# A mixer's elementwise work on one Trainium2 core: GpSimd's part moved to VectorE, gate units two slots after slot 2, square roots in fours

## The reference

```
p = z @ w_in_mix                       # xl | gl | u | v, 512 columns each
xc = short_conv(xl)                    # 4 taps
for direction in (forward, backward):
    r, i = sigmoid(xc @ w_r + b_r), sigmoid(xc @ w_i + b_i)   # 8 heads x 64
    log_a = -8 * r * softplus(-lam);  a = exp(log_a)
    b = sqrt(-expm1(2 * log_a)) * (i * xc)
    h = linear_scan(a, b, h0)          # h[t] = a[t] * h[t-1] + b[t]
y_lru = (h_f + h_b) * gelu(gl)
y_sgu = u * (w_s @ layernorm(v) + b_s) # chunks of 128 tokens, 4 groups
out = concat(y_lru, y_sgu) @ w_out_mix
```

## Time and profile before

| what | us |
| --- | --- |
| median of 3 runs | 1647.9 (1644.72 to 1651.6) |
| the profiled execution | 1644.98 |
| its span, first to last instruction | 1643.2 |
| TensorE busy | 1581.4 (96%) |
| VectorE busy | 975.8 (59%) |
| ScalarE busy | 630.3 (38%) |
| GpSimd busy | 176.2 (11%) |

### The profile page before, as it was taken

One profiled execution on the slowest core, in us unless ns is written; L12 is line 12 of the kernel. 1 busy time (PEld: TensorE's weight loads), 2 busy tenths in 40 slices (PEclk: granted clock), 3 DMA queues, 4 the chain that ended last, 5 costly groups with the idle time before them and its releaser, 6 DMA issues.

```text
span 1643.2 us, 24197 instructions
## 1 busy us (share of the span) xinstructions
PE 1581.4 (96%) x8838; PEld 1310.6 (80%) x8838; DVE 975.8 (59%) x1352; ACT 630.3 (38%) x838; POOL 176.2 (11%) x158
## 2 busy tenths in 40 slices
PE   5999999999999999999999999999999998799998
PEld 4788888887777787888888877888888865799997
DVE  6777777223698467773333367773333279865554
ACT  3322222222563353334322242223222247367752
POOL 0000000011343210000001010000000125320001
PEclk9999999999999999999999999999999998999999
DMA  9455556343313435552234335552334332455663
GB/s 375 145 184 186 187 180 191 127 169 114 100 61 123 154 112 173 189 192 89 100 131 153 128 97 185 182 188 89 102 129 154 128 90 90 165 208 191 191 207 114
DMA packets 84187, 249.48 MB, mean 152 GB/s; under 512 B 12704, under 2 KB 13856, under 8 KB 82976
## 3 DMA queue, kind: packets, MB, share of 16 engines
q1 hardware_dynamic: 84128, 248.71, 45.7%
HBM read 247.62 MB, written 1.05 MB: 151 GB/s over the span
## 4 chain that ended last, share of the span: by engine, by line
PE 85%; DVE 6%; issue 3%; DMA 2%; ACT 2%; POOL 2%; DVEq 0%; SPq 0%; POOLq 0%; ACTq 0%
PE bank L335 27%; PE bank L337 26%; PE bank L336 26%; DMA ada_raw<-ada_w 2%; DVE ada_acc L909 1%; PE bank L523 1%; DVE w_lo L754 1%; PE bank L355 1%; ACT z_hi L617 1%; POOL y_lo L1160 1%; DVE w_hi L983 1%; DMA res<-x_t 0%; PE bank L390 0%; DVE l_q L960 0%; DVE l_q L958 0%
## 5 line engine op out<-in xcount | busy, mean ns | idle before, releaser
L754 DVE TENSOR_TENSOR w_lo<-raw,w_hi 128x1024 fp32r<-128x1024 f32 x320 | 398.1, 1244 | 434.2 <-ACT w_hi L591 236.3
L335 PE MATMUL bank<-z_hi,w_hi 128*128 128x512 f32 (+1 forms) x1600 | 586.9, 367 | 10.5 <-DVE z_lo L830 7.3
L336 PE MATMUL bank<-z_lo,w_hi 128*128 128x512 f32 (+1 forms) x1600 | 577.3, 361 | 0.0
L337 PE MATMUL bank<-z_hi,w_lo 128*128 128x512 f32 (+1 forms) x1600 | 577.1, 361 | 0.0
L335 PEld LDWEIGHTS bank<-z_hi,w_hi 128*128 128x128 f32 x1600 | 301.7, 189 | 69.2 <-issue 15.6
L597 ACT ACTIVATE w_hi<-raw 128x1024 fp32r<-128x1024 f32 x176 | 186.6, 1060 | 433.3 <-PE bank L337 432.5
L336 PEld LDWEIGHTS bank<-z_lo,w_hi 128*128 128x128 f32 x1600 | 301.7, 189 | 47.4 <-issue 2.7
L337 PEld LDWEIGHTS bank<-z_hi,w_lo 128*128 128x128 f32 x1600 | 301.4, 188 | 46.9
L591 ACT ACTIVATE w_hi<-raw 128x1024 fp32r<-128x1024 f32 x120 | 127.1, 1060 | 337.7 <-PE bank L337 337.3
L335 PE MATMUL bank<-h_hi,w_hi 128*128 128x512 f32 (+1 forms) x704 | 254.0, 361 | 0.0
L336 PE MATMUL bank<-h_lo,w_hi 128*128 128x512 f32 (+1 forms) x704 | 254.0, 361 | 0.0
(11 more groups left out here) (127 smaller groups left out, 1074.6 us busy)
## 6 DMA issues: line engine op xcount, KB each, us to landing
raw<-weights SPq DMA_DIRECT2D x320, 512.0 KB, 3.3
ada_raw<-ada_w SPq DMA_DIRECT2D x176, 256.0 KB, 3.0
ada_z<-ada_w SPq DMA_DIRECT2D x20, 1024.0 KB, 5.9
ada_head<-head_w SPq DMA_DIRECT2D x8, 1024.0 KB, 20.3
res<-x_t SPq DMA_DIRECT2D x1, 2048.0 KB, 7.9
bd<-gate_w SPq DMA_DIRECT2D x4, 256.0 KB, 4.5
out<-res SPq DMA_DIRECT2D x4, 256.0 KB, 2.2
ws<-sgu_w SPq DMA_DIRECT2D x2, 256.0 KB, 4.8
```

Source lines behind the costliest of these rows:

```text
L335: pe.matmul(bank_ap, w_hi[:, r, c], rhs_hi, start=start, stop=False)
L336: pe.matmul(bank_ap, w_hi[:, r, c], rhs_lo, start=False, stop=False)
L337: return pe.matmul(bank_ap, w_lo[:, r, c], rhs_hi, start=False, stop=stop)
L754: dve.tensor_tensor(w_lo[:, r, :], raw[:, r, :], w_hi[:, r, :].bitcast(F32), ALU.subtract).then_inc(lo_ready, 1)
```

## The change

GpSimd keeps only the 1/sqrt of the statistics. Its two l_bx operations become one VectorE operation, in a new function `coefficients`, which also takes the first step (old L958) out of `scans`. All eight y_lo are made on VectorE, and the output stage takes k in the order 0 to 7. Gate units follow slots 2 to 9; in layer 1 units with d = 1 use the banks pa[2:4], so that TensorE waits for ti_ready of two units back. ScalarE takes the square roots in fours, exp before the second tanh, the weight copies of all q but 6 to 9, gelu at q = 11, and y_hi inside q = 14 and 15. VectorE's scans stand at q = 6, 7, 11 and 12, scans(0) and scans(1) before the wait for the slot. Of xpad only the edges are zeroed, of bd only the off-diagonal blocks; the gate transfers no longer wait, conv(0) waits for the edges (pad_zero), and TensorE's first gate product for bd_zero. The core of the diff:

```diff
-Y_ORDER = (4, 0, 1, 5, 2, 3, 6, 7)
-Y_POOL = 6
+GATE_LAG = 2
-MIX_HI_DVE = range(4, 16)
+MIX_HI_DVE = range(6, 10)
...
+        def gate_banks(l, u):
+            return pa[2:4] if l == DEPTH - 1 and u % 2 else [p_ada, p_misc]
...
-                        sp.wait_ge(bd_zero, l + 1)
...
+                sets = 2 if wl == SEQ else 1
...
-                    if 4 <= q < 12:
-                        u = q - 4
+                    if GATE_LAG <= q < GATE_LAG + 8:
+                        u = q - GATE_LAG
                         t_, d_ = u // 2, u % 2
                         pe.wait_ge(xc_ready, 4 * l + t_ + 1)
                         if u == 0:
                             pe.wait_ge(mix_in, 64 * (l + 1))
+                            pe.wait_ge(bd_zero, l + 1)
                             pe.wait_ge(mods_ready, MODS0 + AT["norm", n]["mod"] + 1)
-                        if u or l:
-                            pe.wait_ge(ti_ready, 8 * l + u)
-                        for kind_, dst in ((0, p_ada), (1, p_misc)):
+                        if u >= sets:
+                            pe.wait_ge(ti_ready, 8 * l + u - sets + 1)
+                        for kind_, dst in enumerate(gate_banks(l, u)):
                             m = pe.matmul(dst[:], bd[:, kind_ * 8 + d_ * 4 + t_, :], xc[:, t_, :], start=True, stop=True)
...
-                for n_, k in enumerate(Y_ORDER):
-                    if n_ < Y_POOL:
-                        pe.wait_ge(y_lo_pool, Y_POOL * l + n_ + 1)
-                    else:
-                        pe.wait_ge(y_lo_dve, (KD - Y_POOL) * l + n_ - Y_POOL + 1)
+                for k in range(KD):
+                    pe.wait_ge(y_lo_ready, KD * l + k + 1)
                     for q in range(2):
...
-                        elif t == 0:
-                            act.wait_ge(bd_zero, l + 1)
...
-                    if 4 <= q < 12:
-                        u = q - 4
+                    if GATE_LAG <= q < GATE_LAG + 8:
+                        u = q - GATE_LAG
                         t_, d_ = u // 2, u % 2
                         c = l * 8 + d_ * 4 + t_
                         r = u % 4
+                        g_r, g_i = gate_banks(l, u)
                         act.wait_ge(gate_mm, 8 * l + u + 1)
                         if u >= 4:
                             act.wait_ge(scan_ready, 4 * l + t_ - 1)
                         elif u == 0:
                             act.wait_ge(lam_ready, 3)
-                        act.activation(l_q[:, r, :], p_ada[:], ACT.Tanh, bias=half_b[:, 0, c:c + 1], scale=0.5).then_inc(act_chain, 1)
-                        act.activation(l_bx[:, r, :], p_misc[:], ACT.Tanh, bias=half_b[:, 1, c:c + 1], scale=0.5).then_inc(ti_ready, 1)
+                        act.activation(l_q[:, r, :], g_r[:], ACT.Tanh, bias=half_b[:, 0, c:c + 1], scale=0.5).then_inc(act_chain, 1)
+                        act.activation(l_bx[:, r, :], g_i[:], ACT.Tanh, bias=half_b[:, 1, c:c + 1], scale=0.5).then_inc(ti_ready, 1)
                         act.wait_ge(act_chain, 2 * (8 * l + u) + 1)
+                        act.activation(l_a[:, r, :], l_q[:, r, :], ACT.Exp, bias=lam_t[:, 5, c:c + 1],
+                                       scale=lam_t[:, 5, c:c + 1]).then_inc(exp_ready, 1)
                         act.activation(l_s[:, r, :], l_q[:, r, :], ACT.Tanh, bias=lam_t[:, 4, c:c + 1],
                                        scale=lam_t[:, 4, c:c + 1]).then_inc(act_chain, 1)
-                        act.activation(l_a[:, r, :], l_q[:, r, :], ACT.Exp, bias=lam_t[:, 5, c:c + 1],
-                                       scale=lam_t[:, 5, c:c + 1]).then_inc(exp_ready, 1)
-                        if d_ == 1:
-                            for u_ in (u - 1, u):
+                        if u % 4 == 3:
+                            for u_ in range(u - 3, u + 1):
                                 act.wait_ge(act_chain, 2 * (8 * l + u_) + 2)
                                 act.activation(l_s[:, u_ % 4, :], l_s[:, u_ % 4, :], ACT.Sqrt).then_inc(sqrt_ready, 1)
-                    if q == 12:
+                    if q == 11:
...
-                for n_, k in enumerate(Y_ORDER):
-                    act.wait_ge(y_ready, 8 * l + n_ + 1)
-                    src = y_lru if k < 4 else y_sgu
-                    act.activation(y_hi[:, k, moving(wl)], src[:, k % 4, 0:wl], ACT.Copy).then_inc(y_hi_ready, 1)
+                    if q == 14:
+                        act.wait_ge(scan_ready, 4 * (l + 1))
+                    for k in {14: (0, 1), 15: range(2, KD)}.get(q, ()):
+                        act.wait_ge(y_ready, 8 * l + k + 1)
+                        src = y_lru if k < 4 else y_sgu
+                        act.activation(y_hi[:, k, moving(wl)], src[:, k % 4, 0:wl], ACT.Copy).then_inc(y_hi_ready, 1)
...
+                if t == 0:
+                    dve.wait_ge(pad_zero, l + 1)
...
+            def coefficients(l, u):
+                r = u % 4
+                dve.wait_ge(ti_ready, 8 * l + u + 1)
+                link(dve.scalar_tensor_tensor(l_bx[:, r, :], l_bx[:, r, :], 1.0, xc[:, u // 2, :], ALU.add, ALU.mult))
+                dve.wait_ge(exp_ready, 8 * l + u + 1)
+                dve.wait_ge(act_chain, 2 * (8 * l + u) + 2)
+                link(dve.scalar_tensor_tensor(l_q[:, r, :], l_a[:, r, :], 1.0, l_bx[:, r, :], ALU.add, ALU.mult))
...
+            def y_low(l, k, wl):
+                src = y_lru if k < 4 else y_sgu
+                dve.wait_ge(y_hi_ready, 8 * l + k + 1)
+                dve.tensor_tensor(y_lo[:, k, moving(wl)], src[:, k % 4, 0:wl], y_hi[:, k, moving(wl)].bitcast(F32),
+                                  ALU.subtract).then_inc(y_lo_ready, 1)
...
                 for q in range(IN_SLOTS):
+                    s = at["slot"] + q + 4
+                    if q in (6, 7):
+                        scans(l, q - 6)
                     dve.wait_ge(slot_done, at["slot"] + q + 1)
-                    s = at["slot"] + q + 4
                     if q in MIX_HI_DVE:
                         dve.wait_ge(raw_in[q % 4], 16 * (s // RING + 1))
                         dve.tensor_copy(w_hi[:, q % 4, :], raw[:, q % 4, :]).then_inc(hi_ready, 1)
-                    if q < 4:
+                    if q < 2:
                         conv(l, q)
-                    split_lo(s, q % 4)
+                        if q == 1:
+                            split_lo(s - 1, 0)
+                            split_lo(s, 1)
+                    elif q < IN_SLOTS - 1:
+                        split_lo(s, q % 4)
+                    if q in (2, 3):
+                        conv(l, q)
+                    for u in {2: (0,), 3: (1,), 4: (2,), 5: (3,), 8: (4, 5), 9: (6,), 10: (7,)}.get(q, ()):
+                        if u == 6:
+                            dve.wait_ge(vrstd_ready, l + 1)
+                            for m_ in range(m4):
+                                m = dve.tensor_scalar(v_n[:, m_, :], pa[m_][:], bn2[:, m_, 0:1], tokr[:, m_:m_ + 1],
+                                                      ALU.subtract, ALU.mult)
+                            m.then_inc(vn_ready, 1)
+                        coefficients(l, u)
                     if q == 7:
                         for m_ in range(m4):
@@ -992,42 +1049,31 @@
                         for m_ in range(m4):
                             m = dve.bn_aggr(bn2[:, m_, :], bn6[:, m_, :])
                         m.then_inc(vvar_ready, 1)
-                    if q == 9:
-                        dve.wait_ge(vrstd_ready, l + 1)
-                        for m_ in range(m4):
-                            m = dve.tensor_scalar(v_n[:, m_, :], pa[m_][:], bn2[:, m_, 0:1], tokr[:, m_:m_ + 1],
-                                                  ALU.subtract, ALU.mult)
-                        m.then_inc(vn_ready, 1)
-                    if q in (6, 8, 10, 12):
-                        scans(l, (q - 6) // 2)
-                    if q >= 12:
-                        g = q - 12
-                        dve.wait_ge(spatial_mm, 4 * l + g + 1)
-                        src = (p_ada, p_misc)[g % 2][:, 0:wl].rearrange("p (m j) -> p m j", j=P)
-                        o = y_sgu[:, g, 0:wl].rearrange("p (m j) -> p m j", j=P)
-                        c = C_SGU + l * LT + g
-                        if g == 0:
-                            dve.wait_ge(mix_in, 64 * (l + 1))
-                        dve.scalar_tensor_tensor(o, src, par[:, c:c + 1], bs[:, g, :].unsqueeze(1).to_broadcast([P, m4, P]),
-                                                 ALU.mult, ALU.add).then_inc(zz_ready, 1)
-                        for n_ in {0: (), 1: (0, 1, 2), 2: (3, 4, 5), 3: (6, 7)}[g]:
-                            k = Y_ORDER[n_]
-                            if k < 4:
-                                dve.wait_ge(gelu_ready, 4 * l + k + 1)
-                                dve.wait_ge(scan_ready, 4 * l + k + 1)
-                                y, factor = y_lru, gl[:, k, 0:wl]
-                            else:
```

(80 more changed lines are left out.)

24 lines of the change are left out of this document (21 added, 3 removed).

## The result

| | before | changed |
| --- | --- | --- |
| median of 4 runs each | 1646.78 us | 1630.51 us (1627.2 to 1635.06) |
| profiled execution, span | 1643.2 us | 1625.4 us |

What follows compares the result with a forecast made beforehand. TensorE was taken to bound layer 0 and VectorE, stretched by GpSimd, layer 1. Gains of 3.3 and 14.8 us sum to 18.1: 1626.9 from the profiled 1645.0, 1629.8 from the median, given as 1630, range 1622.5 to 1639.

Steps and rivals of the forecast that it cites:

- The sign on the clock: Expected mark of a right forecast: TensorE's granted clock above 0.85 over layer 1's fullest stretch.
- The stretch, 18 us: VectorE's queue in layer 1: 87.2 us against a clean 69.2, the 18 us laid to GpSimd's operations beside it.
- Clean prices and the queue: VectorE in layer 1: unstretched operation times put the new queue up to the last y_lo at 70.3 us.
- The start: Layer 1's first convolution comes 1.6 us earlier without the wait for full zeroing, 0.7 if the edges cost as much.
- New waits: VectorE in layer 1 waits for weight copies, coefficients, the first square root and the last gate: together 4.4 us.
- The end of layer 1: y_lo 7 ends at 1413.2, TensorE's last six matmuls add 0.9, giving 1414.1 against 1428.9: 14.8 us gained.
- Layer 0: TensorE bounds it; the y products end at 528.9 against 532.2, a gain of 3.3 us.
- Gate 5's cover: Layer 0: ScalarE's unit 4 is done at 464.9, before TensorE arrives at 465.2, a cover of 0.3 us.
- A (hand-offs): Rival: waits in the gates' loop of TensorE, ScalarE and VectorE take 8 us of the gain: 1638, chance 0.12.
- the 5 of the sign: Expected mark of the hand-off rival: waits on ScalarE past 5 us in sum.
- B (layer 0 stalls): Rival: gate 5's cover fails and units 5 to 7 follow some 2 us late each: 1634, chance 0.08.
- C: Rival: VectorE's stretch has a cause other than GpSimd and stays, so moved work costs more: 1656, chance 0.03.

Runs made afterwards that it cites:

- e3: Changed kernel with two additions of 512 columns, which nobody waits for, on GpSimd behind each unit's ti_ready: 1639.27 us.
- e4: Changed kernel with six fillings of 512 columns, which read nothing and nobody waits for, on GpSimd behind each unit: 1631.95 us.
- e2: Changed kernel with the l_bx step put back on GpSimd as two operations: 1636.94 us.
- e1: Kernel before with only the l_bx step moved from GpSimd into VectorE's scans(), as one operation: 1637.98 us.
- e6: Changed kernel with gate units behind slots 4 to 11 again and scans and coefficients moved later to match: 1643.80 us.
- e7: Changed kernel with ScalarE's square roots after every second unit in place of fours: 1630.93 us.
- e10: Kernel before with only xpad's edges and bd's off-diagonal blocks zeroed, and no bd_zero wait for gate transfers and ScalarE's first copy: 1644.59 us in one run.
- e5: Changed kernel with y_lo of k = 0 to 5 put back on GpSimd, in the new order of k: 1628.16 us.
- e8: Changed kernel with spatial_gate(0) ahead of scans(3), y_hi 2 and 3 at q = 14, y_lo 2 and 3 ahead of spatial_gate(3): 1633.13 us.
- e12: e8 with 12 and 16 idle products of constants on TensorE in layer 1, ahead of the last spatial product's wait and y_lo 0's: 1627.13 us.

## Why the prediction was right, step by step

- **What bounds.** TensorE in layer 0, VectorE in layer 1: right. In e3 VectorE's busy time grew by 11.8 us in layer 0, which took 122.55 us against 122.59, and by 14.6 in layer 1, which grew by 10.6. The sign on the clock came too: 0.93 in the changed kernel over 1366 to 1400, and 0.95 over the same part of the stage, 5.9 us earlier, where it was 0.85.
- **The stretch, 18 us.** Right, and shown by e3 and e4; forecast from durations beside and away from GpSimd. GpSimd's two small rstd steps, 0.5 us in the sum, stretched nothing that the rows show. Two slips, neither in the forecast's sum: the old order's clean terms add up to 69.5, not 69.2, so the stretch was 17.7 us; and it didn't strike VectorE's operations "whatever their kind". Of the products of the kernel before, the pair with both factors in SBUF took 0.76 us alone and 1.30 beside GpSimd, and the pair with one factor in a bank of PSUM 0.73 beside it:

```profile
1416.88 0.76 DVE L1024 TENSOR_TENSOR y_lru<-y_lru,gl 128x256 f32<-128x256 f32 x2
...
1420.14 1.30 DVE L1024 TENSOR_TENSOR y_lru<-y_lru,gl 128x256 f32<-128x256 f32 x2
...
1424.59 0.73 DVE L1024 TENSOR_TENSOR y_sgu<-y_sgu,bank 128x256 f32<-128x256 f32 x2
```

GpSimd is at its y_lo from 1420.39 on.
- **Clean prices and the queue.** I had y_lo 7 75.2 us after the first convolution (70.3 + 4.4 + 0.5). It ended 75.0 after it.
- **The start.** 1.6 us forecast; 19.85 to 18.22 from tok. GpSimd's two fillings of the edges take 0.11 and 0.10 us:

```profile
422.25 0.11 POOL L1198 MEMSET xpad<- 128x8 f32 x1
422.30 0.10 POOL L1199 MEMSET xpad<- 128x4 f32 x1
```

- **New waits.** 4.4 us forecast, 4.50 measured, at the places named: w_lo 7 (1.00), w_lo 9 (0.46), coefficients 3 (1.41), first root 1.22, the last gate 0.41.
- **The end of layer 1: the term that was mis-sized.** I let TensorE's last six matmuls follow y_lo 7 by 0.9 us. In fact it got y_lo 2 at 1406.46 and from there had 36 matmuls of its own, so the result came 1.8 us after y_lo 7. It had waited only 0.23 us for y_lo 2: from the third spatial product at 1399.51 on TensorE has hardly a gap, so its own work behind the bank, slot 15 partly at the low clock, ends layer 1 almost as much as y_lo 2 does. The gain in layer 1 was 13.8 us, not 14.8.
- **Layer 0.** 3.3 us forecast, 3.29 measured. The eight gates stay 7.20 us apart. Gate 5's cover is 0.5 us, from ScalarE's tanh ending at 465.1 to the gate at 465.58:

```profile
464.40 0.68 ACT L685 ACTIVATE l_bx<-bank,half_b 128x512 f32<-128x512 f32 x1
```

- **Sum.** 18.1 us, of which the two mixers gave 17.1. The median fell on the forecast partly by luck: its own executions spread over 8 us, the medians differ by 16.3, and the median of the kernel before, now over four executions, lies 1.1 us below the 1647.9 that the forecast started from.
- **Rivals.** A (hand-offs) didn't come: TensorE waits 0.2 us for gate results, and VectorE 4.1 us in sum on ScalarE, below the 5 of the sign. B (layer 0 stalls) didn't come here, nor in e2. C is refuted by e1, e2 and e3. What I had not seen at all is how much the early gates carry (e6): in the sum they had a cost, in waits, and no gain.

By the runs, GpSimd's l_bx step is about half of layer 1's 13.8 us: clearing it alone gives 6.6 (e1), and putting it back takes 7.0, 1.8 of it in waits (e2). Roots in fours give 2.9 (e7), the start 0.8 (e10) and y_lo 0.9 (e5). Taking the lag back, with what hangs on it, costs 6.8 (e6). The parts don't add up, since each moves what is late next.

## What to carry to other kernels

If an engine seems full, compare one operation's duration where its neighbour is quiet and where it isn't. A second length that goes with the neighbour's activity points to contention; a run like e3, with work on the neighbour that nobody waits for, can show it, and moving work onto the full engine can then shorten it, as here. A reordering can move a wait to a worse place: in e8 the wait right ahead of TensorE's last run of products cost the clock on top, while in the changed kernel the low clock fell on slot 15, where it cost little. And a schedule that packs one engine's work (roots in fours, copies) needs its inputs early; take the two as one edit.

## What the runs showed of the hardware that I had not expected

- With GpSimd busy for 26 us either way, operations that read lengthened VectorE's two coefficient steps (two inputs) from 0.69 to 1.2 us on average (e3), and fillings not at all (e4); a one-input weight copy of 1024 columns went from 0.68 to 0.92 beside the first and 0.79 beside the second.
- After waits of 2.36 and 2.58 us close together TensorE ran its next 4 us at a granted clock of 0.50, with its 256-column matmuls 0.21 us apart in place of 0.12 (e8); idle products of constants in both gaps kept it at 1.00 (e12).
- Two profiled executions (e2 and e7) had a granted clock of 0.91 in the norm ahead of layer 1's mixer, and were 0.9 us longer there, at a place where their instructions are those of the others. I don't know why.
- Two others (e6 and e8) took 222 us from layer 1's first result to the end of the span, where the changed kernel took 215, though nothing was edited there and the granted clock was 1.00 over the bulk of it: 1360 matmuls in e8's 1440 to 1600 us against 1412 in the changed kernel's. Why is open. The 7 us are about as much as the executions of one kernel spread.
